# Expert rows gathered into a ring of ten slots instead of eight

## The reference

```python
def peer_ffn(u, wq, k1, k2, eu, ev):
    ...
        q = (xc @ wq).reshape(PEER_CHUNK, PEER_HEADS, 2, half)
    ...
        top_s, pos = lax.top_k(cand, PEER_TOPK)
        eidx = jnp.take_along_axis(cidx, pos, -1)
        g = jax.nn.softmax(top_s, -1).astype(xc.dtype)
        h = jax.nn.gelu(jnp.einsum('thkd,td->thk', eu[eidx], xc), approximate=False)
        return jnp.einsum('thk,thkd->td', g * h, ev[eidx])
```

## Time and profile before

| | us |
|---|---|
| median of 3 runs | 3073.07 (3072.62 to 3074.68) |
| span of the profiled execution | 3069.2 |
| its own time beside the median | the span is 3.9 below it |

### The profile page before, as it was taken

How to read it: one execution, slowest core, us unless ns; L and a number is a source line. 1 busy time by engine, 2 the same in 40 slices (tenths; PEclk the granted TensorE clock), 3 DMA queues, 4 the chain that set the end, 5 groups by cost and what they waited for, 6 DMA issues and landing times.

```text
span 3069.2 us, 34666 instructions
## 1 busy us (share of the span) xinstructions
PE 2401.4 (78%) x11912; PEld 1303.6 (42%) x11912; DVE 1920.4 (63%) x6197; ACT 452.5 (15%) x1108; POOL 730.7 (24%) x779
## 2 busy tenths in 40 slices
PE   7989995878999778568889888877797566665565
PEld 6778891433555435124545543322695111120111
DVE  3879977876544547857854455555458855555555
ACT  2141120233000111012010012221221000000000
POOL 0000002222222222323322223332001323333332
PEclk8999996878999879667989987665897555566556
DMA  8628748998999978878999999998535989999997
GB/s 327 241 105 326 279 170 348 356 364 331 407 407 395 382 301 351 336 301 350 388 390 418 404 382 377 381 379 350 190 130 190 353 328 399 399 387 401 397 401 301
DMA packets 155375, 1029.85 MB, mean 336 GB/s; under 512 B 19136, under 2 KB 29888, under 8 KB 34496
## 3 DMA queue, kind: packets, MB, share of 16 engines
q0 software_dynamic: 110592, 805.36, 65.9%
q1 hardware_dynamic: 31648, 209.70, 17.5%
q10 hardware_dynamic: 12960, 12.59, 1.2%
HBM read 1018.66 MB, written 8.91 MB: 335 GB/s over the span
## 4 chain that ended last, share of the span: by engine, by line
PE 48%; DMA 22%; DVE 18%; issue 4%; POOL 4%; ACT 2%; ACTq 0%; DVEq 0%; SPq 0%; POOLq 0%
DMA ring<-in_peer_uv,eT 21%; PE PS L1368 13%; DVE ring L2533 8%; PE PS L928 6%; PE PS L1387 6%; POOL ring L746 4%; PE PS L1039 4%; PE PS L850 4%; PE PS L1012 2%; PE PS L949 2%; PE PS L969 1%; PE PS L1221 1%; PE PS L813 1%; PE PS L1121 1%; DMA xr<-xrows 1%
## 5 line engine op out<-in xcount | busy, mean ns | idle before, releaser
L2533 DVE CUSTOM_DVE_ANT_0 ring<-ring,PS 128x512 f32<-128x512 f32 x1536 | 994.0, 685 | 825.6 <-PE PS L1387 506.2
L746 POOL DMA_INDIRECT ring<-in_peer_uv,eT x768 | 728.8, 949 | 2309.7 <-PE PS L1368 1463.3
L1387 PE MATMUL PS<-xr,onesb 3*128 3x512 bf16 x1536 | 536.5, 484 | 457.0 <-DVE hcol L2533 372.1
L1368 PE MATMUL PS<-ring,zcol 128*32 128x512 f32 x3072 | 580.6, 895 | 97.9 <-DVE zcol L2543 95.9
L1387 PEld LDWEIGHTS PS<-xr,onesb 3*128 3x128 bf16 x1536 | 105.8, 95 | 997.2 <-DVE hcol L2533 534.0
L1368 PEld LDWEIGHTS PS<-ring,zcol 128*32 128x32 f32 x3072 | 102.7, 142 | 382.0 <-issue 216.8
L928 PE MATMUL PS<-uT,W 128*128 128x256 f32 x1024 | 247.0, 390 | 0.0
L1837 ACT ACTIVATE ge<-hdot 128x4 f32<-128x4 f32 x192 | 39.4, 205 | 1302.0 <-DVE hdot L2538 1301.8
L928 PEld LDWEIGHTS PS<-uT,W 128*128 128x128 f32 x1024 | 192.2, 193 | 48.1 <-issue 22.2
L1910 DVE CUSTOM_DVE_ANT_0 ring<-ring 128x1024 f32<-128x1024 f32 x160 | 190.3, 1222 | 7.6 <-DMA ring<-in_w_rows 3.5
L850 PE MATMUL PS<-uT,W 128*128 128x256 f32 (+1 forms) x672 | 155.7, 385 | 8.0 <-ACT uT L1451 7.6
(11 more groups left out here) (362 smaller groups left out, 2283.4 us busy)
## 6 DMA issues: line engine op xcount, KB each, us to landing
ring<-in_w_rows SPq DMA_DIRECT2D x40, 1024.0 KB, 8.0
W<-in_w_in SPq DMA_DIRECT2D x30, 1024.0 KB, 9.8
W<-in_w_gate SPq DMA_DIRECT2D x16, 1408.0 KB, 8.4
W<-in_w_gate SPq DMA_DIRECT2D x16, 1280.0 KB, 7.7
W<-in_w_out SPq DMA_DIRECT2D x20, 1024.0 KB, 5.1
W<-in_w_gate SPq DMA_DIRECT2D x16, 1152.0 KB, 10.1
ring<-in_w_q SPq DMA_DIRECT2D x16, 1024.0 KB, 14.2
ring<-in_peer_uv,eT POOLq DMA_INDIRECT x768, 10.2
```

The costliest lines, as they stand in the source:

```text
L746: pool.indirect_dma_start(ring[:, slot, :], None, (peer_uv0, peer_uv1)[b.l], bass.IndirectOffsetOnAxis(eT[:, f % 2, t:t + 1], 0)).then_inc ...
L1368: last = T.matmul(PS[k * NR:(k + 1) * NR, (6 + h) * 512:(7 + h) * 512], zcol[:, g % 2, k, NR - 1 - at:2 * NR - 1 - at], ring[:, slot, D + ...
L1387: T.matmul(bank(x_bank(q, n) + h), onesb[p0:p0 + 3, :], xr[p0:p0 + 3, g % 2, h * 512:(h + 1) * 512], start=True, stop=True)\
L2533: V.tensor_tensor_reduce(out=u_half, in0=u_half, in1=bank(x_bank(q, n) + h), scale=1.0, scalar=0.0, op0=ALU.mult, op1=ALU.add, accum_out=h ...
```

## The change

The ring gets ten slots. `QUERY_SLOTS = 8` keeps the number of query weight tiles. A token's slot is now its number over all three streams modulo ten, so the streams no longer begin at slot 0 (LAT1 begins at token 512, slot 2), and a gather waits for `wo` only if its slot held a query tile. `LEAD` goes from 6 to 8. The 16 KB per partition come from: the descriptor reserve, set to 4096 bytes (12,288 freed); `silu_c`, now a view of ring slot 8 (1,024); `ones`, one column that the matmul reads 128 times with step 0 (508); and `sg`, now a view of the inner part of `hpad` (2,048).

```diff
-SLOTS = 8
+SLOTS = 10
+QUERY_SLOTS = 8
...
-LEAD = 6
+LEAD = 8
...
         ring = sb("ring", [P, SLOTS, 2 * D])
+        silu_c = part(ring[:, QUERY_SLOTS, :], 0, [KD, 32])
...
-        sg = sb("sg", [P, 2, TOK])
+        sg = hpad[:, :, TAPS // 2:TAPS // 2 + TOK]
...
-        ones = sb("ones", [P, P])
+        ones = sb("ones", [P, 1])
...
-        silu_c = sb("silu_c", [P, KD, 32])
...
-        query_land = [sem(f"query_weights_landed{k}") for k in range(SLOTS)]
+        query_land = [sem(f"query_weights_landed{k}") for k in range(QUERY_SLOTS)]
...
         def slot_of(q, n):
-            return n % SLOTS, 16 * (q * (TOK // SLOTS) + n // SLOTS + 1)
+            whole = q * TOK + n
+            return whole % SLOTS, 16 * (whole // SLOTS + 1)
...
-                for t in range(SLOTS):
+                for t in range(QUERY_SLOTS):
...
-                if b.apart and n < SLOTS:
-                    pool.wait_ge(a["wo"], a.at("wo", TT * KD + 16 + 2 * n + 2))
                 t = token(n // GRP, n % GRP)
                 slot, _ = slot_of(q, n)
+                if b.apart and n < SLOTS and slot < QUERY_SLOTS:
+                    pool.wait_ge(a["wo"], a.at("wo", TT * KD + 16 + 2 * slot + 2))
...
-                    last = T.matmul(bank(at, 0, TOK), ones[:, :], hacc[:, q, :], start=(q == 0), stop=(q == 1))
+                    last = T.matmul(bank(at, 0, TOK), ones[:, 0:1].to_broadcast([P, P]), hacc[:, q, :], start=(q == 0), stop=(q == 1))
...
-                    last = T.matmul(bank(at, TOK, 2 * TOK), ones[:, :], hsq[:, q, :], start=(q == 0), stop=(q == 1))
+                    last = T.matmul(bank(at, TOK, 2 * TOK), ones[:, 0:1].to_broadcast([P, P]), hsq[:, q, :], start=(q == 0), stop=(q == 1))
...
-    nc = bacc.Bacc("TRN2", target_bir_lowering=False, num_devices=1)
+    nc = bacc.Bacc("TRN2", target_bir_lowering=False, num_devices=1, dynamic_dma_scratch_size=4096)
```

## The result

| | before | after |
|---|---|---|
| median, us | 3072.85 (4 runs, 3067.36 to 3074.68) | 3030.39 (4 runs, 3029.32 to 3031.7) |
| ratio, with its 95% interval | | 0.9874 (0.986 to 0.9889) |
| span of the profiled execution | 3069.2 | 3029.9 |

The kernel is 42 us faster; the forecast was 3029.

What follows compares the result with a forecast made beforehand. No engine is full; DMA limits beside gate weights, late gathers the last stretch, PE and DVE elsewhere. Gains of 26 + 12 + 6 = 44 us gave 3073 - 44 = 3029 us, range 2998 to 3062.

Steps and rivals of the forecast that it cites:

- 26 + 12 + 6 = 44: Microseconds gained: 26 with experts almost alone (2480 to 3050), 12 beside attention (1830 to 2140), 6 beside gate weights.
- The failed step: Last stretch, 2480 to 3050 us: a group's cycle falls from 10.5 to 10.0 us, 26 us over 52 groups.
- little for the x rows: Last stretch: allowance for x rows and uneven engines, between 9.96 us for four full-rate gathers and the forecast 10.0.
- The dips: Last stretch: slow slices just behind request bursts, 268 to 393 GB/s, read as engines running dry between requests.
- Rival B: Packets behind a burst stay slow because POOL's writing of requests slows the engines; gain 19 us, 3054; chance 20%.
- pure lateness of the first landing: Last stretch: the part still gained if packets stay slow behind bursts, 0.2 us a group, 10 us.
- Rival D: Another wait takes its place: x rows land later behind more gathers, cycle stays 10.5 us; 3065 to 3073; chance 8%.
- Beside the gate weights: 760 to 1060 and 1485 to 1830 us: two gathers fetched early, 3 us each, 6 together; bounds 0 and 29.
- Beside the attention: 1830 to 2140 us: a longer queue removes half of 25.1 us of DVE's gather waits, 12 us; bounds 0 and 25.
- The zeros: Parts forecast at 0 us: LEAD, wo wait, descriptor reserve, ones, sg, silu_c, and stretches where DVE hardly waits for gathers.
- the first kind: 475 to 760 and 1060 to 1485 us, also 2340 to 2480: PE and DVE set the pace; gain 0.

Runs made afterwards that it cites:

- experiment 4: Changed kernel without the x row loads from LAT1's group 16 on (old rows broadcast): 3005.55 us, ratio 0.9781.
- experiment 1: Changed kernel with eight slots, LEAD 6 and silu_c in its own memory again; reserve 4096, ones and sg as changed: 3070.7 us, ratio 0.9997.
- (6): Changed kernel with plain loads of consecutive rows by SP's queue in place of POOL's gathers from token 576 on: 3024.51 us, ratio 0.9865.
- (7): Changed kernel where a gather also waits until the gather six before it has landed, so requests are spread out: 3027.98 us, ratio 0.9876.
- (5): Changed kernel where POOL gathers 128 consecutive rows in place of scattered ones from token 576 on: 3030.61 us, ratio 0.9878.
- Experiment 10: Changed kernel with x row packets of 64 bytes in place of 1 KB from LAT1's group 16 on: 3006.62 us, ratio 0.9799.
- experiment 12: Changed kernel with a group's x rows in two loads of 12 partitions, one for each half, in place of four of 3: 3011.19 us, ratio 0.981.
- experiment 3: Changed kernel where tokens 400 to 511, beside layer 1's attention, wait as if there were eight slots: 3039.21 us, ratio 0.9891.
- 8: Changed kernel with a descriptor reserve of 1024 bytes in place of 4096: 3028.49 us, ratio 0.9873.
- 2: Changed kernel where gathers from token 560 on, the last stretch, wait as if there were eight slots: 3040.32 us, ratio 0.9905.

## Why the prediction was right, and where it was wrong

**The total was right through two errors that cancel,** and that was luck. 26 + 12 + 6 = 44 was forecast; the same stretches gave 9 + 12 + 16 = 37, and 2 more came from places forecast at 0, which is within scatter.

**The failed step** is "a cycle should fall from 10.5 us to four gathers at the full rate, 4 x 2.49 = 9.96, plus a little for the x rows and uneven engines: 10.0". Its first half holds: with the x rows gone, experiment 4 has 9.94 in most groups, 10.11 on average, and 421 GB/s. The "little for the x rows" is what failed. It was never worked out, and it is 0.43 us, nearly all that the step meant to gain. The kernel before has the x rows on three engines too, and its even cycles take 10.5 us already, so these probably set the pace there too. The uneven engines were sized too small as well, at 0.04 for both: experiment 4 is 0.15 above 9.96. The earlier trace rows was read too quickly as well. The dips were put down to too few requests, but where the engines that are ahead must stop for those behind, the sum over 16 engines dips too, and no view of single engines told the two apart. (Nor were three older gathers out when POOL made its request at 2865.61: by their landings, at 2867.73 and 2870.16, there were two.) More depth lets the leading engines run further ahead (1 gather before, 2.8 after) and gives those behind nothing. It removed only what was a late first row (longest wait 2.6 to 1.2 us), and that was small: 9 to 14 us for the stretch. About 4 of these fall in its first five groups and 2 to 4 at the turn of the tile, the two places where the forecast saw no gain, and only 1 to 2 in the 24 groups of the steady part.

**Rival B** described the last stretch: landing 4.4 us later, the rate there 400 where it was 395, with the "pure lateness of the first landing" priced at 10 us, about what was measured. That it comes to the same is partly luck: the price was 0.2 us in every group, but the cycle fell by 0.09 (0.05 against experiment 1), and the rest came at the start and the turn of the tile. Its cause was wrong as well. It blamed POOL's writing of requests; without any (6), spread out (7) and with neighbouring rows (5), the cycle is 10.54 to 10.60. **Rival D** named the x rows, but as loads that land late and that PE waits for. Experiment 10 still has PE waiting for x rows, 34.3 and 18.5 us from 2480 to 2990 us (the changed kernel 47.1 and 33.5), at a cycle of 10.08. In experiment 12 PE hardly waits for them, 0.7 us, and the cycle is still 0.22 above 10.11. So it is the DMA time of these loads that costs, not their lateness.

**Beside the gate weights** the mechanism was right and the size off: two more gathers fetched early in each stretch, 3 us each. The term measured 7 and 9. Each stretch already gains more than the 5 us of two early gathers. DMA share rose from 0.99 and 0.98 to 1.00 and the rate from 402 to 410 and 412, so besides the early rows the engines had idle time within these stretches that a longer queue fills. The forecast named that and valued it at nothing because PE is 90% busy. PE's business was no obstacle: DVE's waits for gathers fell by 43 and 17 us. With eight slots (experiment 1) the two stretches are 285 and 346 us again, so the gain is the slots'. That the rate is the way it comes about is argued from these rows; no run undid the depth in these stretches alone.

**Beside the attention** 12 us was forecast as half of 25 us of waits, and 12 came; in experiment 3 the trace gives 12 back, its run times 5 to 9. But the reasoning was only partly so: the waits went to 0.2, all of them, and half of their time was spent on something else.

**The zeros** held: the first kind (-2 and 0), the reserve (experiments 1 and 8), `ones` and `sg` (experiment 1). `silu_c` had its own memory back in experiment 1 and was not run alone, nor was `LEAD`. The 4 us between groups 127 and 139 are scatter: experiment 1, with eight slots, takes 350.6 us there, the changed kernel 350.5.

**What stays open.** Shown is that packets of 1 KB in these loads cost the 0.43 us (4, 10), that two slots more or less move the cycle by less than 0.1 beside them (10.54, and 10.59 and 10.60 in 1 and 2), and that three engines carry them and fall behind (the chains above, and experiment 12, where 12 engines share them). Not shown is why the 8 KB packets beside them take 4 to 27 ns longer. That the instruction packets make the long groups of experiment 4 is read from their order in time alone. Eight slots without x rows and more than ten slots were not tried.

## What to carry to other kernels

When a queue reads 0.99 busy and still falls short of its best rate, list everything that passes through it before adding depth, and price the smallest stream too, by the engine that carries most of it: here 0.6% of the bytes took 4% of the cycle. Deeper prefetch pays where the consumer's waits are long and irregular (12 and 16 us here), and hardly where a saturated stream sets a steady cycle (9 to 14 us of 554, most of them not in the steady part). Before a layout is made wider for the DMA's sake, see what the layout did for the matmul: two short matmuls in different groups of 32 partitions take 0.39 us a pair, and in the same one 0.60.

## What the runs showed that was not expected

- 24 packets of 1 KB a group, in four loads to three partitions each, all go over the same three of 16 engines and lengthen a cycle of 10.11 us to 10.54 beside 4 MB of 8 KB packets; the same 24 packets in two loads to 12 partitions go over 12 engines and lengthen it to 10.33 only, and packets of 64 bytes by 0.1 at most.
- Small packets also lengthen the large ones beside them: 8 KB packets take 314 ns on average without them, 319 with 24 packets of 1 KB a group spread over 12 engines, and 341 with 128 over 16.
- A reserve of 1024 bytes held some six gathers in flight without a request of POOL's taking over 0.954 us from 760 to 1055 us.
- The same 1 MB tiles come at the same steady rate by POOL's scattered gathers, by gathers of neighbouring rows and by plain loads of SP's queue: 10.54, 10.60 and 10.54 us a group.
